# Low-rank mixer stage of a two-block layer: masked blocks in two buffers, empty places in the woven order, and a third output tile beside the closing norm

## The reference, cut to what matters

```
proj = x @ w_in                                   # 22 column blocks of 128
sa    = einsum('bhij,bhj->bhi', state, -kk)
state = state * decay + sa (x) (kk * a) + v (x) k  # one step per token
out   = einsum('bhij,bhj->bhi', state, r)
y = group_norm(out) ; y = (y + bonus) * g
mixed = concat([pool_out, y]) @ w_out
h = layer_norm(alpha * x + mixed, ln1_g, ln1_b)    # then router logits, experts
```

## Time and profile before

| | |
|---|---|
| median of three runs | 3975.98 us |
| the profiled execution, its own time | 3975.18 us |
| its span, first to last instruction | 3973.3 us |
| PE busy | 3694.7 us, 93% |
| DVE, ACT, POOL busy | 1669.5, 1193.1, 502.0 us |
| mean granted TensorE clock | 0.969 |
| mixers and output stage | about 0 to 1045 us of the span |

### The profile page before, as it was taken

The page is one execution under the profiler, slowest core; times in us unless marked ns, Lnnn a source line. Parts: engine busy times, 40 slices in busy tenths (PEclk is TensorE's granted clock), DMA queues, the critical chain, the costliest instruction groups (busy, mean ns, idle before and its releaser), DMA issues.

```text
span 3973.3 us, 57089 instructions
## 1 busy us (share of the span) xinstructions
PE 3694.7 (93%) x24715; PEld 2278.9 (57%) x24715; DVE 1669.5 (42%) x2602; ACT 1193.1 (30%) x2133; POOL 502.0 (13%) x491
## 2 busy tenths in 40 slices
PE   8899999988799999898999999997899999999999
PEld 4465565564377777444555555554455566556664
DVE  2444555443411111463444444444223555456541
ACT  1323333321011111233333333333222444334430
POOL 0212121111100000231100110100111100120000
PEclk9899999998799999999999999998999999999999
DMA  3000000022489999980000000002010000000001
GB/s 104 22 17 18 18 18 16 28 94 96 165 332 365 365 370 366 348 281 11 17 16 17 17 17 17 9 4 104 32 71 0 11 1 1 13 22 1 1 18 68
DMA packets 109201, 346.81 MB, mean 87 GB/s; under 512 B 13478, under 2 KB 39398, under 8 KB 90774
## 3 DMA queue, kind: packets, MB, share of 16 engines
q1 hardware_dynamic: 87014, 284.85, 19.8%
q0 software_dynamic: 9072, 33.03, 2.4%
q10 hardware_dynamic: 12864, 25.27, 1.8%
HBM read 296.94 MB, written 46.19 MB: 86 GB/s over the span
## 4 chain that ended last, share of the span: by engine, by line
PE 81%; DVE 9%; ACT 3%; issue 3%; POOL 2%; DMA 2%; SPq 0%; POOLq 0%; ACTq 0%; DVEq 0%
PE ps L2573 9%; PE ps L1644 8%; PE ps L398 8%; PE ps L2051 7%; PE ps L2078 7%; PE ps L3284 7%; PE ps L1661 4%; PE ps L2591 4%; PE ps L3556 3%; PE ps L2966 3%; PE ps L1172 3%; PE ps L3237 2%; PE ps L2282 1%; POOL sb L1856 1%; PE ps L494 1%
## 5 line engine op out<-in xcount | busy, mean ns | idle before, releaser
L2573 PE MATMUL ps<-sb 128*128 128x512 f32 x960 | 468.1, 604 | 28.8 <-ACT sb L1973 10.2
L2051 PEld LDWEIGHTS ps<-sb 128*128 128x128 f32 x2624 | 289.7, 142 | 320.0 <-ACT sb L2059 154.4
L2051 PE MATMUL ps<-sb 128*128 128x128 f32 x2624 | 425.3, 285 | 31.9 <-ACT sb L2059 21.4
L2059 ACT ACTIVATE sb<-ps 128x512 f32<-128x512 f32 x336 | 200.5, 597 | 714.3 <-PE ps L2051 714.3
L2035 ACT ACTIVATE sb<-ps,sb 128x1280 f32<-128x1280 f32 (+1 forms) x288 | 353.3, 1231 | 115.8 <-DVE sb L2028 112.2
L2066 DVE COPY sb<-ps 128x512 f32<-128x512 f32 x320 | 220.2, 688 | 357.3 <-PE ps L2051 356.2
L398 PE MATMUL ps<-sb 128*128 128x512 f32 x704 | 364.3, 633 | 4.6 <-DMA sb<-in_w_in 3.0
L1644 PE MATMUL ps<-sb 128*128 128x256 f32 x1504 | 342.8, 381 | 0.8 <-ACT sb L1676 0.8
L3284 PE MATMUL ps<-sb 96*128 96x512 f32 (+1 forms) x768 | 333.3, 527 | 9.0 <-DVE sb L3341 7.2
L2078 PEld LDWEIGHTS ps<-sb 128*64 128x64 f32 x5248 | 288.2, 138 | 72.0 <-issue 38.1
L2078 PE MATMUL ps<-sb 128*64 128x128 f32 x5248 | 323.1, 278 | 4.3 <-DVE sb L2066 4.1
(11 more groups left out here) (365 smaller groups left out, 4687.8 us busy)
## 6 DMA issues: line engine op xcount, KB each, us to landing
sb<-in_exp_gate SPq DMA_DIRECT2D x47, 1024.0 KB, 6.9
sb<-in_exp_up SPq DMA_DIRECT2D x47, 1024.0 KB, 9.6
sb<-in_exp_down SPq DMA_DIRECT2D x47, 1024.0 KB, 13.5
sb<-in_l_w_mod ACTq DMA_DIRECT2D x12, 2048.0 KB, 13.2
d_ys<-sb SPq DMA_DIRECT2D x47, 512.0 KB, 14.1
sb<-d_x SPq DMA_DIRECT2D x32, 512.0 KB, 3.9
sb<-in_w_in SPq DMA_DIRECT2D x22, 512.0 KB, 4.2
sb<-in_x SPq DMA_DIRECT2D x16, 512.0 KB, 6.6
```

The source lines that it names most:

```text
L2051: ins = k.pe.e.transpose(k.bank(6)[:, 128 * j:128 * j + 128], self.Pb[g % 2][:, 1280 * b + 128 * c:1280 * b + 128 * c + 128], k.f(C_ID, 128))
L2573: ins = pe.e.matmul(k.bank(5), lhs[:, kk, :], w[:, kk, 512 * half:512 * half + 512], start=kk == 0, stop=kk == 7)
```

## The change

Four things.

1. The masked block of level lv lies in buffer lv % 2: `Mk`, or the columns 64 to 128 of `TT`. POOL writes the masks of levels 0 and 1 both at the step of level 0, and at the step of level lv the mask of level lv + 1, when the product of level lv - 1 has read that buffer (for level 2, when DVE too has read level 0's). The mask of level 1 waits for the end of the round before's scan.
2. A step `("gap",)`, in which no engine does anything, stands before `join` in each group's list, and two of them between the two `lora_mm`. They move what is woven against them.
3. Fourteen products of output tile 2 (seven for each half) are woven with the closing norm, in banks 6 and 7, and left out in `out_and_norm`, where tile 2 is left with its eighth product, as tiles 0 and 1 are.
4. The router product moves from bank 6 to bank 4.

```diff
+    masked_block = (Mk, TT[:, :, 64:128])
...
-        return out + [("join", g), ("join_a", g), ("join_b", g)]
+        return out + [("gap",), ("join", g), ("join_a", g), ("join_b", g)]
...
-        return [("lora_mm", f, 0), ("lora_mm", f, 1), ("decay", f), ("decay_p", f)]
+        return [("lora_mm", f, 0), ("gap",), ("gap",), ("lora_mm", f, 1), ("decay", f), ("decay_p", f)]
...
-            order += [("scan_end",)] + finish(f)[:-1]
+            order += [("scan_end",)] + weave(finish(f)[:-1], [("out", 2, half, kk) for half in range(2) for kk in range(7)])
...
-            pe.wait_ge(*t["mk", g])
+            pe.wait_ge(*t["mk", g, lv])
...
-                ins = pe.e.matmul(M_(g)[at_, e, i, :], Mk[halves[h], u, :], right, ...)
+                ins = pe.e.matmul(M_(g)[at_, e, i, :], masked_block[lv % 2][halves[h], u, :], right, ...)
...
-            t["mm", g] = t["mmt", g] = product.at
+            t["mm", g] = t["mk free", g, lv % 2] = product.at
...
-                t["TT", g] = t["mmt", g] = evac_v.at
+                t["TT", g] = t["mk free", g, 0] = evac_v.at
...
-            pool.wait_ge(*t["mmt", g])
-            pool.e.tensor_tensor(Mk[:, lu, :], zb[g][:, :, 0:64], bc(k.f(C_LV + 64 * lv, 64), 1, 8), ALU.mult)...
-            t["mk", g] = pool_out.at
+            for level in (0, 1) if lv == 0 else (lv + 1,) if lv < 5 else ():
+                pool.wait_ge(*t["mk free", g, level % 2])
+                if level == 1:
+                    pool.wait_ge(*t["scan_end"])
+                pool.e.tensor_tensor(masked_block[level % 2][:, lu, :], zb[g][:, :, 0:64], bc(k.f(C_LV + 64 * level, 64), 1, 8), ALU.mult)...
+                t["mk", g, level] = pool_out.at
...
+    def bank(self, n, half):
+        return 6 + half if n == 2 else 2 * (n % 2) + half
...
-        pe, b = self.k.pe, 2 * (n % 2) + half
+        pe, b = self.k.pe, self.bank(n, half)
...
-            for kk in range(max(4 * part, 0 if n > 1 else 7), 4 * part + 4):
+            for kk in range(max(4 * part, 0 if n > 2 else 7), 4 * part + 4):
...
-            pe.wait_ge(*free[6])
+            pe.wait_ge(*free[4])
...
-                ins = pe.e.matmul(k.bank(6)[:, 0:36], hT[n % 2][:, kk, :], wr[:, kk, :], start=kk == 0, stop=kk == 7)
+                ins = pe.e.matmul(k.bank(4)[:, 0:36], hT[n % 2][:, kk, :], wr[:, kk, :], start=kk == 0, stop=kk == 7)
```

More of the change, by code:

```diff
@@ L282, in mixers @@
     for g in range(2):
-        for n in ("mm", "mmt", "T", "TT", "M free"):
+        for n in ("mm", "T", "TT", "M free"):
             t[n, g] = FREE
+        t["mk free", g, 0] = t["mk free", g, 1] = FREE
         t["ym", g] = FREE
@@ L474, in pe_program @@
                 right = idc[halves[h], :] if lv == 0 else Tm[halves[h], u, :]
-                ins = pe.e.matmul(M_(g)[at_, e, i, :], Mk[halves[h], u, :], right, start=True, stop=True, skip_group_check=True)
+                ins = pe.e.matmul(M_(g)[at_, e, i, :], masked_block[lv % 2][halves[h], u, :], right, start=True, stop=True, skip_group_check=True)
             ins.then_inc(*product.up())
-            t["mm", g] = t["mmt", g] = product.at
+            t["mm", g] = t["mk free", g, lv % 2] = product.at
         elif kind == "merge_b":
@@ L985, in pool_ahead @@
             pool.wait_ge(*t["zb", g])
-            pool.wait_ge(*t["mmt", g])
-            pool.e.tensor_tensor(Mk[:, lu, :], zb[g][:, :, 0:64], bc(k.f(C_LV + 64 * lv, 64), 1, 8), ALU.mult).then_inc(*pool_out.up())
-            t["mk", g] = pool_out.at
+            for level in (0, 1) if lv == 0 else (lv + 1,) if lv < 5 else ():
+                pool.wait_ge(*t["mk free", g, level % 2])
+                if level == 1:
+                    pool.wait_ge(*t["scan_end"])
+                pool.e.tensor_tensor(masked_block[level % 2][:, lu, :], zb[g][:, :, 0:64], bc(k.f(C_LV + 64 * level, 64), 1, 8), ALU.mult).then_inc(*pool_out.up())
+                t["mk", g, level] = pool_out.at
         elif kind == "scan_r":
@@ L1284, in dve_program @@
             dve.wait_ge(*t["mm", half])
-            dve.e.scalar_tensor_tensor(out=hr[s][:, hs], in0=xr[s][:, hs], scalar=ALPHA, in1=k.bank(2 * s + half), op0=ALU.mult, op1=ALU.add).then_inc(*evac_v.up())
-            free[2 * s + half] = t["sum"] = evac_v.at
+            dve.e.scalar_tensor_tensor(out=hr[s][:, hs], in0=xr[s][:, hs], scalar=ALPHA, in1=k.bank(ahead.bank(n, half)), op0=ALU.mult, op1=ALU.add).then_inc(*evac_v.up())
+            free[ahead.bank(n, half)] = t["sum"] = evac_v.at
         elif kind == "norm":
@@ L1299, in dve_program @@
             dve.wait_ge(*t["rows"])
-            dve.e.tensor_tensor(lg[:, x[0], :], k.bank(6)[:, 0:36], br, ALU.add).then_inc(*evac_v.up())
-            free[6] = evac_v.at
+            dve.e.tensor_tensor(lg[:, x[0], :], k.bank(4)[:, 0:36], br, ALU.add).then_inc(*evac_v.up())
+            free[4] = evac_v.at
     def pool_program(kind, *x):
```

## The result

The changed kernel took 3940.76 us (median of four runs, 3935.49 to 3944.16) beside 3974.71 us for the kernel before (median of four, 3970.16 to 3976.08): a ratio of 0.9915, interval 0.9898 to 0.9933. The profiled execution took 3941.0 us over a span of 3939.2. The prediction was 3942 us, in a range of 3927 to 3958.

What follows compares the result with a forecast made beforehand. PE, busy 93% of the span, was taken as the bound. Terms 11.6 + 1.7 + 7.6 + 1.4 + 5.5 + 6 = 33.8 us off 3975.2, with the median 0.8 above, gave 3942 us; range 3927 to 3958.

Steps and rivals of the forecast that it cites:

- Clock: Half-clock stretches behind waits the change shortens: a third of their cost returns, 6 us, between a loss of 6 and 17.
- before round 0: While the second low-rank product waits for ACT, two more projections get done: 1.7 us.
- round 0: Waits for the level 1 and level 3 masks and at `lora_mm` 1 shrink, joins come later: 7.6 us.
- rounds 1 to 4, clean: Per round without the clock, 1.3 us from masks and 1.6 from empty places; 11.6 us over four rounds.
- round 5: No projections to fill with and no `lora_mm`, so only the mask gains: 1.4 us.
- output stage: Fourteen tile 2 products move beside the closing norm, delaying it but shortening the stage: 5.5 us, between 3.5 and 9.1.
- Masks: Level 1 product of the second group, rounds 1 to 4: starts 1.3 us earlier, still waiting for L868.
- The blocked rival: POOL's second mask holds DVE's L828 back in every round, taking the masks' gain: 3951 us, chance 0.15.
- Empty places: Rounds 1 to 4: the second low-rank product starts 1.6 us earlier, with new waits at the scan and `kk_sum`.
- the chain of 7.2 us: Rounds 1 to 4: `kk_sum` starts a fixed 7.2 us behind the second low-rank product, `lora_mm` 1.
- Third tile: Tile 2's fourteen products beside the closing norm: exponentials start 3.5 us later, transposes of `h` wait for POOL; gain 5.5 us.
- The rival of new waits that pull the clock down: Scan waits lower the clock in four rounds and tile 2 stays at half clock: 3954 us, chance 0.15.

Runs made afterwards that it cites:

- one place: The changed kernel with one empty place instead of two between the two `lora_mm`: 3939.32 us, ratio 0.9927.
- masks and places: The changed kernel without the third output tile's part, the router product staying in bank 4: 3944.61 us, ratio 0.9925.
- cover, mixed places: The changed kernel with one `lora_mm` gap in rounds 1 to 4, tile 2's products split between closing norm and layer norms, later transposes: 3916.23 us.

## Why the prediction was right, step by step

The predicted terms against what the trace of the changed kernel shows to L1458. "Clock" is what is left of the whole when the other terms are taken off, with the predicted 1.7 and 7.6 kept for the two stretches in which no profile has a full clock; it is worked out, not read.

| term | predicted | shown |
|---|---|---|
| before round 0 | 1.7 | 3.5, with the clock from 0.92 to 0.94 behind 100 us |
| round 0 | 7.6 | 15.2, with the clock from 0.92 to 0.99 |
| rounds 1 to 4, clean | 2.9 each | 2.5 (round 2) |
| round 5 | 1.4 | 1.2 for the mask; with the clock down from 0.93 to 0.90 the round lost 1.1 |
| output stage | 5.5 | 5.8, of which 3.3 come without the tile too (below) |
| clock | 6 (-6 to 17) | 37.0 - 1.7 - 7.6 - 10.0 - 1.2 - 5.8 = 10.7 |
| behind the output stage | 0 | a loss of 2.9 |

*Masks.* Right to 0.1 us: 1.3 predicted, 1.3 and 1.2 where they stand alone. In round 5 the first level 1 product starts 777.11 - 771.07 = 6.04 us behind rk, for 810.69 - 803.41 = 7.28. The reading that decided it was that the product waits for L868 as well, so that the idle time of 1.82 was not the gain. The blocked rival is out: L830 took 1.94 us at most, and POOL's second mask waited instead. The Trainium skill ("SBUF — State Buffer", section "Who interferes with whom") says that issue order decides who blocks; it has no case of two GpSimd instructions with a VectorE one between them. Here the VectorE instruction that was already waiting when the first mask ended went first, in all six rounds.

*Empty places.* The mechanism was right, the chain of 7.2 us is 7.16 in three kernels, and the waits moved to the scan as named. The size was 0.4 too large, 2.5 - 1.3 = 1.2 us for 1.6: join 1 (L506) to the second low-rank product took 581.98 - 573.47 = 8.5 us for 8.3, and the join came 0.2 us later than put. The new waits in round 3 are 1.32 and 0.83 us, for 1.5 and 1.1. What the prediction missed is that its own chain of fixed length makes the second place a loss: it stood in the sum that ACT needs 3.9 us and PE had 4.8 of work. With one place ACT is just not late, and a round gives 0.86 more.

*Round 0.* 15.2 us for 7.6. The clean part can't be split from the clock to better than a microsecond or two: by the windows the kernel before spent (1 - 0.92) x 2 x 134 = 21 us at half clock there and the changed one (1 - 0.99) x 2 x 118 = 2. Half of the difference is 9.5 us, by which 5.7 would be left. What is shown is that the waits named went: the masks' 4.9 us, of which 0.6 for L870 stayed, and the low-rank product's 1.0; a wait of 0.7 for ACT is new. Either part alone already took the long wait of 3.07 us for POOL. With the empty places alone it was gone, with the masks alone a wait of 1.8 us for DVE's L886 stood there. So the masks were not needed for that term.

*Third tile.* The times were forecast from the first mean's start, 31.15 us earlier than in the earlier trace rows: transposes at 927.5 (shown 896.38 + 31.15 = 927.53), the second ones at 938.9 (907.76 + 31.15 = 938.91), exponentials 10.6 us behind the mean (880.20 - 869.61 = 10.6). One reading was off: the second wait of the transposes was named as some 2 us and is 4.75. And the value of the term depends on the clock that it is compared with. Masks and places without the tile gained 3.3 us in this stretch all the same (closing exponentials 32.8 ahead, L1458 36.1), and with the tile 5.8. The two kernels without the tile have the same code here; the stretches are 908 to 938 us of before and the same 30 us of masks and places:

```profile
908.00:938.00 30.00, 17.50 (x43) 10.22 (x44) 15.12 (x25) 2.27 (x4) 5.82 (x4) 0.66 0.16 60
```

```profile
875.50:905.50 30.00, 17.91 (x52) 9.62 (x53) 15.82 (x26) 1.91 (x4) 5.82 (x4) 0.77 0.19 69
```

(0.77 - 0.66) x 2 x 30 = 6.6 us less at half clock, of which half is the 3.3. So the tile was worth 5.8 us against a stage in which the clock was low for long, as in the kernel before, and 2.5 against one in which it was not. The prediction's 5.5 was worked out against the rows of the kernel before, so it holds for the first.

*Clock.* 10.7 us for 6, inside the ends given. It was the largest single error: how many falls go. The term was put for the whole; most of it came in round 0 (15.2 - 7.6 = 7.6 us, if the 7.6 hold) and it turned negative in rounds 3 and 5. The rival of new waits that pull the clock down was right in kind: beside the counts above, the window behind the scan's wait of 1.32 us in round 3 of the changed kernel,

```profile
585.00:595.00 10.00, 7.84 (x33) 4.38 (x31) 4.14 (x7) 3.16 (x4) 1.61 (x4) 0.83 0.00 0
```

has the only fall of that round. That the forecast came within 1.3 us of the median is partly luck: the terms without clock were 1.5 us too large, the clock 4.7 too small, and 2.9 were lost behind the stage, where none was forecast: 33.8 - 1.5 + 4.7 - 2.9 = 34.1 us, the shown difference of the spans. A second profile of the same kernel had 26.7. What the reasoning earned is the mechanism, the price of a clean round and the range.

## What to carry to other kernels

Before a wait is credited with its idle time, ask what the same instruction waits for next, and what is pinned to it further on: here a mask's 1.82 us was worth 1.3, and an empty place that hid a wait delayed the scan behind it by as much as it was too long. Filler that is moved into one hole is missing from the next: fourteen products beside the closing norm were worth 2.5 to 5.8 us, and the same fourteen split over both holes, with later transposes, 19 more. Compare versions at the end of the stage that was changed, by trace, not only by medians. And look first at how far two profiles of the same code differ there (here up to 3.6 us) before a smaller difference is given a cause.

## What the runs showed of the hardware

The same code behind L1458, 15,146 matmul records on PE, took from 2912.7 us (masks and places) to 2928.5 us (cover, mixed places) in the twelve profiles. Windows over it, of these two kernels:

```profile
1019.00:3931.00 2912.00, 2746.24 (x15146) 1710.48 (x15145) 1197.17 (x1806) 899.81 (x1584) 321.06 (x331) 0.98 0.29 104
```

```profile
989.00:3917.00 2928.00, 2762.53 (x15146) 1721.59 (x15146) 1197.33 (x1807) 899.26 (x1584) 320.53 (x331) 0.97 0.28 103
```

The 16 us are in PE's busy time, with the clock 0.98 and 0.97. Two profiles of one and the same kernel, the changed one, already differ by 6.9 us there. So the granted clock makes more difference in this untouched part than several terms of this change.

One and the same wait, 1.8 us for the level 1 mask, was followed by a lower clock in 8 of 12 rounds and left it at 1.00 in the other 4, in part in the same code. At 1.3 us it was followed by none in 36. A fall cost some 1.7 us (3.4 us at half clock, worked out above), as much as the wait. So the price of a wait is not its own length alone, and it is an average over executions.

Two masks of 1.28 us on POOL, with a DVE instruction of two SBUF inputs waiting, took 3.49 us, 0.93 more than alone: the second mask paid, and the DVE instruction took 1.94 us, for 1.93 beside one mask.
